# Expert weights fetched in 2 MB transfers into pairs of neighbouring places, with the first loads in a new order

## The chip, the cores and the metric

One Trainium2 chip, one of its cores. The metric is the device time of one execution in microseconds; lower is better. Before and after are compared by the median of several executions.

## The reference, cut to what matters

One step of a one-layer decoder trunk in float32 for 520 tokens (512 of a prompt, 8 samples), width 1024. After a first half (three mixers between an input and an output projection) comes a mixture of 32 experts, of which every token uses 4:

```
logits = xt @ router_w + router_b;  top_v, top_i = top_k(logits, 4);  top_w = softmax(top_v)
for each block of rows with one expert e:
    g = min(x @ w_gate[e] + b_gate[e], 7);  u = clip(x @ w_up[e] + b_up[e], -7, 7)
    y = ((u + 1) * g * sigmoid(1.702 * g)) @ w_down[e] + b_down[e]
x = x + g2 * sum over a token's 4 experts of top_w * y
```

`w_gate`, `w_up` and `w_down` are 1024 x 1024 float32 for each of the 32 experts: 96 matrices of 4 MB, 384 MB in all. Each is read once.

## The kernel before, in words

TensorE does all products. In its first part (to about 285 us in the profile) the kernel computes the mixers, the output projection, the second norm and the routing. Then it goes through 32 expert steps s = 0..31. The expert of a step is the one whose rank by number of tokens is `ORDER[s]`; steps with many tokens have more blocks (`WIDTH` 2 to 5: 64, 64+32, 64+64 and 64+64+32 token rows), so their work on TensorE is longer, while each needs the same 12 MB of weights. Experts 0 and 1 are taken first, so that their weights can be fetched before the routing is known.

**Chunks.** Every matrix comes in four chunks of 1 MB, 8 KB for each of the 128 partitions. Of gate and up, partition p holds the eight rows 8p to 8p + 7, and chunk j brings two neighbouring ones of them (`(p q k) n`, q = 4, k = 2); of down, chunk j brings 256 neighbouring rows, two for each partition (`(q p k) n`). Either way a partition's 8 KB are one run in memory. Chunk numbers run 0..383: gate and up of expert 0 (0 to 7), then in each later step gate, up (8 chunks) and the down matrix of the step before (4 chunks). Chunk n goes to buffer `n % 18` (`NBUF = 18`); `PLACE` says which 8 KB column of memory each buffer is. Twelve of these columns (`raw`) serve the first part's weights and other tiles before, six (`raw2`) lie elsewhere; columns 5, 6, 7 and 1 (`X2_SLOTS`) hold `x2` and broadcasts until the second norm has been written out.

**Issue.** SyncE (SP) issues all weight transfers in one order in one queue, `fetch` and `m_load` (line 489). Chunks 0 to 2 (`EARLY`) are issued once some small results are in; chunks up to 14 (`MIDDLE`) once the output projection is done with its weights (and, for the columns of `X2_SLOTS`, once `x2` has been spilled to DRAM and the norm is ready); 15 to 17 once the routing logits are there. Every later chunk n waits until TensorE has used chunk n - 18: `sp.wait_ge(m_used, n - NBUF + 1)`.

**Use.** In `project` (gate, up) and `down`, TensorE waits for the chunk's own semaphore `m_full[slot]`, multiplies (line 1917, all blocks), and adds one to `m_used`. So chunk follows chunk strictly in order, three passes for a step: gate(s), up(s), down(s-1), with transposes (L1580) and bias products (L1907, L1911) in between.

**Other traffic in these steps.** GpSimd (POOL) gathers the token rows of the next experts from `h2_d` (h_scratch) into `xrow` with indirect DMAs (L673, rows of 4 KB), and scatters results to `y_d` (y_scratch). The first gather starts when the routing of the first two experts is known, after `h2_spill` (the norm's rows written by ScalarE's queue, L975); TensorE's first transpose of the expert steps (L1580, psum<-ident,xrow) waits for it.

Of the kernel before, what the change touches and what calls it, by code (L numbers as in the profile page):

```python
# [26 lines left out]
E, K, DFF = 32, 4, 1024  # L27
# [18 lines left out]
NBUF = 18  # L46
# [44 lines left out]
def blocks_before(s):  # L91

    return sum(len(BLOCKS[w]) for w in WIDTH[:s])
# [8 lines left out]
PRM_LOADS, BC_LOADS = 34, 3  # L102
X2_SLOTS = (5, 6, 7, 1)

EARLY, MIDDLE = 3, 15
PLACE = (15, 16, 17, 0, 2, 3, 8, 9, 10, 11, 6, 7, 4, 1, 5, 12, 13, 14)
CODES = TT * K
FIRST = 96
WIN_ORDER = [1, 2, 3, 5, 0, 4, 6]
# [10 lines left out]
def trunk_program(nc, x_prompt, x_sample, state_pool, state_conv, state_lru_conv, state_lru_h, c_prompt, c_sample,  # L120
# [123 lines left out]
    with ctx:  # L244
        psum = ctx.enter_context(nc.psum_tensor("psum", [P, 8, 512], F32))
        bk = [psum[:, i, :] for i in range(8)]
# [9 lines left out]
        def sem(name):  # L256
            return ctx.enter_context(nc.semaphore(name))
# [6 lines left out]
        m_full = [sem(f"m_full{i}") for i in range(NBUF)]  # L264
        m_used = sem("m_used")
# [94 lines left out]
        def buf(n):  # L360
            at = PLACE[n]
            return raw[:, at, :] if at < 12 else raw2[:, at - 12, :]

        def first_chunk(s):

            return 12 * s - 4 if s else 0
# [31 lines left out]
        def extras(eng, cycle):  # L398

            n = eng.value_load(task_i[0:1, N_AT:N_AT + 1], min_val=0, max_val=XTRA)  # L400
            with eng.Fori(0, XTRA // 8) as q:
                with eng.If(q * 8 < n):
                    with eng.Fori(q * 8, q * 8 + 8) as more:
                        with eng.If(more < n):
                            cycle(more)
            return n
# [16 lines left out]
        def _(sp):  # L423
# [30 lines left out]
            for kind, c in LOADS:  # L454
                kh, n = slice(4 * (c % 2), 4 * (c % 2) + 4), c // 2 + (4 if kind == "mod" else 0)
# [18 lines left out]
                sp.dma_start(bias_raw[E * r:E * r + E, 0, :], moe_b_gate[0, :, h]).then_inc(bias_loaded, 16)  # L474
                sp.dma_start(bias_raw[E * r:E * r + E, 1, :], moe_b_up[0, :, h]).then_inc(bias_loaded, 16)

            def rows_of(mat, e, j):

                down = mat is moe_w_down
                order = "(q p k) n -> p q k n" if down else "(p q k) n -> p q k n"  # L480
                sizes = dict(q=4, k=2)
                if isinstance(e, int):
                    m = mat[0, e].rearrange(order, **sizes)
                    return m[:, j, :, :]
                m = mat[0, bass.ds(e, 1)].rearrange("o " + order.replace("p q k n", "p (o q) k n"), **sizes)
                return m[:, j, :, :]

            def m_load(slot, src):
                sp.dma_start(buf(slot).rearrange("p (k n) -> p k n", k=2), src).then_inc(m_full[slot], 16)  # L489

            def expert(s):

                if s < 2:
                    return s
                return sp.value_load(task_i[0:1, ORDER[s]:ORDER[s] + 1], min_val=0, max_val=E - 1)

            def fetch(n, src):

                if n < EARLY:
                    sp.wait_ge(mod_out[0], 256)  # L500
                    sp.wait_ge(mod_out[1], 256)
                elif n < MIDDLE:
                    sp.wait_ge(chunk_used, C_MOE)
                    if PLACE[n] in X2_SLOTS:
                        sp.wait_ge(x2_spill, 16 * TT)
                        sp.wait_ge(h2_ready, TT)
                elif n < NBUF:
                    sp.wait_ge(logit_ps, TT)
                    sp.wait_ge(mask_done, 1)
                    sp.wait_ge(h2_spill[0], 48)  # L510
                    sp.wait_ge(h2_spill[1], 32)
                else:
                    sp.wait_ge(m_used, n - NBUF + 1)
                m_load(n % NBUF, src)

            before = None
            for s in range(E):
                if s == 2:
                    sp.wait_ge(ids_done, 1)
                e = expert(s)  # L520
                for c in range(8):
                    fetch(first_chunk(s) + c, rows_of((moe_w_gate, moe_w_up)[c // 4], e, c % 4))
                if s:
                    for c in range(4):
                        fetch(first_chunk(s) + 8 + c, rows_of(moe_w_down, before, c))
                before = e
            for c in range(4):
                fetch(first_chunk(E) + c, rows_of(moe_w_down, before, c))
# [1 line left out]
            def extra(q):  # L530

                e = sp.value_load(task_i[0:1, bass.ds(q + E, 1)], min_val=0, max_val=E - 1)
                for c in range(12):
                    sp.wait_ge(m_used, q * 12 + (12 * E + c - 11))
                    m_load((12 + c) % NBUF, rows_of((moe_w_gate, moe_w_up, moe_w_down)[c // 4], e, c % 4))

            sp.wait_ge(all_tables, 1)
            n = extras(sp, extra)


# [1029 lines left out]
        def _(pe):  # L1570
# [322 lines left out]
            def turn_rows(b, rows, full, evicted, count):  # L1893

                pe.wait_ge(x_rows[b], full)
                if evicted is not None:
                    pe.wait_ge(aT_a, evicted)
                    pe.wait_ge(xg_a, count)
                    pe.wait_ge(xg_d, count)
                for k in range(KC):  # L1900
                    last = turn(bk[6 + k // 4][:, (k % 4) * P:(k % 4) * P + rows], xrow[0:rows, b, k:D:KC], rows)
                last.then_inc(xt_ps, 1)

            def bias(out, mat, w):

                if w == 64:
                    mm(out, sel[:, :], btab[:, mat, :], start=True, stop=False)  # L1907
                else:
                    for g4 in range(4):
                        h, c = g4 // 2, 256 * (g4 % 2)  # L1910
                        mm(out[32 * g4:32 * g4 + 32, :], sel[:, 64 * h:64 * h + 32].bitcast(F32),  # L1911
                           btab[:, mat, c:c + 256].bitcast(F32), start=True, stop=False)

            def products(out, w, x, weights, start, stop):

                for g4 in range(128 // w):
                    last = mm(out[w * g4:w * g4 + w, :], x, weights[:, 8 * w * g4:8 * w * g4 + 8 * w],  # L1917
                              start=start, stop=stop)
                return last

            def project(mat, outs, widths, parts, slot0, full):

                for out, w in zip(outs, widths):
                    bias(out, mat, w)
                for j in range(4):
                    slot = (slot0 + j) % NBUF
                    pe.wait_ge(m_full[slot], full(j))
                    for size in (64, 32)[::(1, -1)[j % 2]]:
                        for kk in range(2):
                            for out, w, (x, at_) in zip(outs, widths, parts):  # L1930
                                if w == size:
                                    last = products(out, w, x[:, 2 * j + kk, at_:at_ + w], buf(slot)[:, D * kk:D * kk + D],
                                                    False, j == 3 and kk == 1)
                    last.then_inc(m_used, 1)
# [16 lines left out]
            def turn_act(widths):  # L1951

                for b, w in enumerate(widths):
                    for j in range(w // 16):
                        last = turn(bk[T_BANKS[b]][:, P * j:P * j + P], act_t[:, b, 256 * (j // 2) + j % 2:256 * (j // 2) + 256:2], P)
                    last.then_inc(at_ps, 1)
# [6 lines left out]
                return [(xb, 0), (xb, 64), (xc, 0)][:len(BLOCKS[w])]  # L1963

            def full_at(c0):
                return lambda j: 16 * ((c0 + j) // NBUF + 1)

            turn_rows(0, GATHERS[0][1], 16, None, None)
            for s in range(E):
                c0, widths, before = first_chunk(s), BLOCKS[WIDTH[s]], blocks_before(s)  # L1970
# [31 lines left out]
            c0 = first_chunk(E)  # L2002
            down([down_bank(E - 1, 0)], (64,), c0, full_at(c0))

            def extra(q):

                def full(c):
                    def count(j):
                        slot = (12 + c + j) % NBUF
                        return q * 16 + 16 * (-(-(12 * E - slot) // NBUF) + 1)  # L2010
                    return count

                pe.wait_ge(y_a, q * 2 + ALL_BLOCKS)
                turn_rows(0, P, q * 16 + 16 * (len(range(0, ALL_TURNS, 2)) + 1), q * 2 + ALL_BLOCKS, q + ALL_TURNS)
                pe.wait_ge(xg_a, q + (ALL_TURNS + 1))
                pe.wait_ge(xg_d, q + (ALL_TURNS + 1))
                pe.wait_ge(sel_done, q + (E + 1))
                both = [(xa, 0), (xa, 64)]
                project(0, (bk[4], bk[5]), (64, 64), both, 12, full(0))
                project(1, (bk[0], bk[1]), (64, 64), both, 16, full(4))  # L2020
                pe.wait_ge(act_done, q * 2 + (ALL_BLOCKS + 2))
                turn_act((64, 64))
                pe.wait_ge(aT_a, q * 2 + (ALL_BLOCKS + 2))
                down((bk[2], bk[3]), (64, 64), 20, full(8))
# [64 lines left out]
```

## Time and profile before

| | us |
|---|---|
| median of 3 runs (lowest, highest) | 1341.56 (1337.92, 1342.29) |
| the profiled execution's own time | 1340.82 |
| its span in the trace | 1339.0 |
| TensorE busy | 1253.5 (94%) |
| granted TensorE clock over the span | 0.96 |
| weights' queue (q1): share of the 16 DMA engines | 85.8% |

TensorE's busy time covers nearly the whole span, and the DMA engines are busy nearly the whole span as well, so neither share says which of them sets the end. For that, one looks where TensorE's idle time is and what ended it, and how full the DMA engines are in each stage.

### The profile page before, as it was taken

What the parts mean: (1) busy time and instruction counts of PE and PEld (TensorE: products, weight loads), DVE (VectorE), ACT (ScalarE), POOL (GpSimd) and SP (SyncE); (2) the same over time, 40 slices, a digit from 0 to 9 for tenths busy, and PEclk for the clock granted to TensorE, in tenths of its full rate; (3) what the DMA queues carried; (4) which work ended last, traced back from release to release, by engine and by line L of the source; (5) the groups of instructions that cost most, each with busy time, mean ns of one, the idle gap of its engine ahead of it and who ended that gap; (6) DMA issues with size and microseconds to landing.
All of it is one profiled execution on the core that took longest, in us unless ns stands there. A gap on an engine that the chain in (4) does not pass through costs nothing.

```text
span 1339.0 us, 19202 instructions
## 1 busy us (share of the span) xinstructions
PE 1253.5 (94%) x8190; PEld 560.8 (42%) x8190; DVE 282.6 (21%) x560; ACT 196.2 (15%) x345; POOL 119.1 (9%) x178
## 2 busy tenths in 40 slices
PE   2899979949999999999999999999999999999976
PEld 1687957733333333333333333333333333333322
DVE  0652874684001000001000000001010010001027
ACT  3514252220000110000000000000001000100022
POOL 3010124010100000000000100000001001000000
PEclk8799988959999999999999999999999999999978
DMA  9654469299999999999999999999999999999974
GB/s 317 199 161 165 152 248 303 89 388 398 352 419 421 421 421 421 409 409 422 407 408 419 420 416 420 421 420 401 416 421 420 421 421 420 422 422 421 421 301 177
DMA packets 95077, 486.43 MB, mean 363 GB/s; under 512 B 13650, under 2 KB 21853, under 8 KB 45303
## 3 DMA queue, kind: packets, MB, share of 16 engines
q1 hardware_dynamic: 83306, 461.15, 85.8%
q0 software_dynamic: 8608, 20.82, 4.2%
q10 hardware_dynamic: 3076, 3.22, 0.7%
q8 instruction: 66, 1.08, 0.3%
q14 instruction: 21, 0.16, 0.0%
HBM read 470.26 MB, written 18.04 MB: 365 GB/s over the span
## 4 chain that ended last, share of the span: by engine, by line
PE 81%; DMA 8%; DVE 5%; SPq 3%; ACTq 1%; ACT 1%; issue 1%; DVEq 0%; POOLq 0%
PE psum L1917 61%; PE psum L1580 4%; PE psum L1575 2%; PE psum L1576 2%; PE psum L1577 2%; DMA raw<-in_moe_w_gate 2%; DMA raw<-in_moe_w_down 2%; SPq L489 2%; PE psum L1907 2%; DMA bd_x<-in_lru_wx 1%; ACTq L766 1%; DMA raw<-in_ada_w 1%; PE psum L2038 1%; PE psum L1737 1%; PE psum L1642 1%
## 5 line engine op out<-in xcount | busy, mean ns | idle before, releaser
L1917 PE MATMUL psum<-raw,xb 128*64 128x512 f32 (+1 forms) x1920 | 304.4, 513 | 0.4 <-DMA raw<-in_moe_w_gate 0.4
L1917 PE MATMUL psum<-raw,aT 128*64 128x512 f32 (+1 forms) x1728 | 301.1, 532 | 3.7 <-DMA raw<-in_moe_w_down 3.5
L1917 PE MATMUL psum<-raw,xa 128*64 128x512 f32 x1280 | 283.5, 595 | 0.0
L1501 DVE TENSOR_SCALAR act_t<-psum 128x512 f32<-128x512 f32 (+1 forms) x46 | 28.4, 642 | 873.4 <-PE psum L1917 873.4
L1917 PEld LDWEIGHTS psum<-raw,xb 128*64 128x64 f32 (+1 forms) x1920 | 100.4, 126 | 189.4 <-issue 175.4
L1917 PEld LDWEIGHTS psum<-raw,aT 128*64 128x64 f32 (+1 forms) x1728 | 98.4, 129 | 187.3 <-issue 167.0
L1917 PEld LDWEIGHTS psum<-raw,xa 128*64 128x64 f32 x1280 | 88.2, 137 | 169.7 <-issue 169.7
L673 POOL DMA_INDIRECT xrow<-h_scratch,gidx x24 | 27.5, 1144 | 464.6 <-PE psum L1580 430.5
L989 ACT ACTIVATE glu<-psum 128x512 f32<-128x512 f32 (+1 forms) x46 | 24.2, 559 | 292.1 <-PE psum L1917 292.1
L1575 PE MATMUL psum<-hT_hi,w_hi 128*128 128x260 f32 x208 | 59.3, 285 | 0.0
L1576 PE MATMUL psum<-hT_lo,w_hi 128*128 128x260 f32 x208 | 58.9, 283 | 0.0
L1577 PE MATMUL psum<-hT_hi,w_lo 128*128 128x260 f32 x208 | 58.7, 282 | 0.0
L685 POOL DMA_INDIRECT y_scratch<-yst_a,sunit x23 | 22.9, 994 | 305.7 <-ACT yst_a L1004 260.4
L1004 ACT ACTIVATE yst_a<-psum 128x512 f32<-128x512 f32 (+1 forms) x27 | 14.5, 558 | 210.3 <-PE psum L1917 210.3
L1642 PE MATMUL psum<-raw,cT 128*9 128x128 f32 x768 | 30.7, 324 | 13.1 <-DMA raw<-in_ada_w 13.1
L1575 PEld LDWEIGHTS psum<-hT_hi,w_hi 128*128 128x128 f32 x208 | 39.1, 188 | 1.1 <-issue 1.1
L1577 PEld LDWEIGHTS psum<-hT_hi,w_lo 128*128 128x128 f32 x208 | 39.2, 189 | 0.0
L1576 PEld LDWEIGHTS psum<-hT_lo,w_hi 128*128 128x128 f32 x208 | 39.1, 188 | 0.1
L1580 PE MATMUL psum<-ident,xrow 128*128 128x128 f32 (+2 forms) x192 | 27.9, 289 | 8.9 <-DMA xrow<-h_scratch,gidx 8.9
L1907 PE MATMUL psum<-btab,sel 128*128 128x512 f32 x76 | 34.3, 478 | 1.1 <-ACT xb L1014 1.1
L1580 PEld LDWEIGHTS psum<-ident,xrow 128*128 128x128 f32 (+2 forms) x192 | 23.5, 198 | 27.7 <-issue 18.7
L1580 PEld LDWEIGHTS psum<-ident,act_t 128*128 128x128 f32 x168 | 22.5, 208 | 27.0 <-issue 25.2
(398 smaller groups left out, 925.2 us busy)
## 6 DMA issues: line engine op xcount, KB each, us to landing
raw<-in_moe_w_gate SPq DMA_DIRECT2D x128, 1024.0 KB, 26.2
raw<-in_moe_w_up SPq DMA_DIRECT2D x128, 1024.0 KB, 26.7
raw<-in_moe_w_down SPq DMA_DIRECT2D x128, 1024.0 KB, 26.9
raw<-in_ada_w SPq DMA_DIRECT2D x24, 1024.0 KB, 8.3
raw<-in_w_in SPq DMA_DIRECT2D x7, 1024.0 KB, 11.5
x<-in_x_prompt SPq DMA_DIRECT2D x2, 2048.0 KB
raw<-in_w_out SPq DMA_DIRECT2D x4, 1024.0 KB, 13.1
yrow_a<-y_scratch SPq DMA_DIRECT2D x2, 2048.0 KB, 10.9
```

The source lines that it names most:

```text
L489: sp.dma_start(buf(slot).rearrange("p (k n) -> p k n", k=2), src).then_inc(m_full[slot], 16)
L673: g.indirect_dma_start(out=out, out_offset=None, in_=h2_d, in_offset=bass.IndirectOffsetOnAxis(ap=index, axis=0), bounds_check=h2_last, oo ...
L685: g.indirect_dma_start(out=out, out_offset=bass.IndirectOffsetOnAxis(ap=index, axis=0), in_=src, in_offset=None, bounds_check=last, oob_is ...
L989: ac.activation(glu[:, b, 0:bank.shape[1]], bank, ACT.Gelu_apprx_sigmoid).then_inc(glu_done, 1)
L1501: v.tensor_scalar(act_t[:, b, 0:bank.shape[1]], bank, 8.0, -6.0, ALU.min, ALU.max).then_inc(u_done, 1)
L1575: mm(out, lhi, rhi, start=start, stop=False)
L1576: mm(out, lhi, rlo, start=False, stop=False)
L1577: return mm(out, llo, rhi, start=False, stop=stop)
L1580: return nc.tensor.transpose(out, src, ident[0:rows, 0:rows])
L1642: last = mm(outs[j], cT[:, 4 * kh + k, :], raw[:, slot, 512 * k + P * j:512 * k + P * j + P], start=False, stop=(kh == 1 and k == 3))
L1907: mm(out, sel[:, :], btab[:, mat, :], start=True, stop=False)
L1917: last = mm(out[w * g4:w * g4 + w, :], x, weights[:, 8 * w * g4:8 * w * g4 + 8 * w], start=start, stop=stop)
```

## The change

Gate and up chunks are fetched two at a time: one transfer of 2 MB puts 16 KB, one run in memory, into each partition, in two neighbouring columns. A partition now holds four consecutive rows of the matrix for a pair (`q=2, k=4`), instead of two for each of two chunks. `PLACE` is reordered so that buffers 0-1, 2-3, ... 16-17 are neighbours. Down chunks stay single, 1 MB. A pair counts on the semaphore of its first buffer; `filled_by` and `fills` work out which semaphore and which count TensorE waits for. A pair waits until both chunks that it overwrites have been used. `EARLY` and `MIDDLE` go from 3 and 15 to 2 and 14, and the first loads are issued in the order of `FIRST_LOADS`. TensorE's products, their order and `m_used` stay.

```diff
-EARLY, MIDDLE = 3, 15
-PLACE = (15, 16, 17, 0, 2, 3, 8, 9, 10, 11, 6, 7, 4, 1, 5, 12, 13, 14)
+EARLY, MIDDLE = 2, 14
+PLACE = (16, 17, 2, 3, 0, 1, 10, 11, 8, 9, 6, 7, 4, 5, 12, 13, 14, 15)
+FIRST_LOADS = (0, 2, 6, 8, 4, 10, 12, 14, 16, 17)
...
+        def buf2(n):
+            at = PLACE[n]
+            whole = raw[:, at:at + 2, :] if at < 12 else raw2[:, at - 12:at - 10, :]
+            return whole.rearrange("p a (k n) -> p (a k) n", k=2)
+        def is_down(c):
+            return c >= first_chunk(E) or (c >= 8 and (c - 8) % 12 >= 8)
+        def filled_by(c):
+            return c % NBUF if is_down(c) else c % NBUF // 2 * 2
+        def fills(c):
+            firsts = [b for b in range(c + 1) if is_down(b) or b % 2 == 0]
+            return sum(filled_by(b) == filled_by(c) for b in firsts)
...
-            def rows_of(mat, e, j):
+            def rows_of(mat, e, j, single=False):
...
-                sizes = dict(q=4, k=2)
+                sizes = dict(q=4, k=2) if down or single else dict(q=2, k=4)
...
+            def m_load2(slot, src):
+                sp.dma_start(buf2(slot), src).then_inc(m_full[slot], 16)
             def fetch(n, src):
+                double = not is_down(n)
...
-                    if PLACE[n] in X2_SLOTS:
+                    if PLACE[n] in X2_SLOTS or (double and PLACE[n] + 1 in X2_SLOTS):
...
-                    sp.wait_ge(m_used, n - NBUF + 1)
-                m_load(n % NBUF, src)
+                    sp.wait_ge(m_used, n - NBUF + (2 if double else 1))
+                if double:
+                    m_load2(n % NBUF, src)
+                else:
+                    m_load(n % NBUF, src)
+            for n in FIRST_LOADS:
+                if is_down(n):
+                    fetch(n, rows_of(moe_w_down, 0, n - 16))
+                else:
+                    fetch(n, rows_of((moe_w_gate, moe_w_up)[n % 8 // 4], n // 8, n % 4 // 2))
...
-                for c in range(8):
-                    fetch(first_chunk(s) + c, rows_of((moe_w_gate, moe_w_up)[c // 4], e, c % 4))
+                for c in range(0, 8 if s > 1 else 0, 2):
+                    fetch(first_chunk(s) + c, rows_of((moe_w_gate, moe_w_up)[c // 4], e, c % 4 // 2))
+                for c in range(2 if s == 1 else 0, 4):
+                    fetch(first_chunk(s) + 8 + c, rows_of(moe_w_down, before, c))
...
-                    pe.wait_ge(m_full[slot], full(j))
+                    pe.wait_ge(m_full[filled(slot0 + j)], full(j))
...
-                return lambda j: 16 * ((c0 + j) // NBUF + 1)
+                return lambda j: 16 * fills(c0 + j)
```

A loop for experts with more tokens than their blocks hold (`extra`) keeps single chunks; its loads and its counts are adapted.

## Rows read from the trace of the kernel before

**Rows 1.** The page: TensorE's busy time, and the DMA engines in 40 slices.

```profile
PE 1253.5 (94%) x8190; PEld 560.8 (42%) x8190; DVE 282.6 (21%) x560; ACT 196.2 (15%) x345; POOL 119.1 (9%) x178
...
DMA  9654469299999999999999999999999999999974
GB/s 317 199 161 165 152 248 303 89 388 398 352 419 421 421 421 421 409 409 422 407 408 419 420 416 420 421 420 401 416 421 420 421 421 420 422 422 421 421 301 177
```

**Rows 2.** Waits of TensorE from 299 to 1284 us: us in total, times, longest.

```profile
PE psum L1917 <- DMA raw<-in_moe_w_down: 3.5, 5, 1.1
...
PE psum L1917 <- DMA raw<-in_moe_w_gate: 0.4, 1, 0.4
```

**Rows 3.** Timeline of TensorE at its waits: start, us, instruction, [idle before].

```profile
294.50 1.55 PE L1580 MATMUL psum<-ident,xrow 96*128 96x96 f32 x8 [8.88 <-DMA xrow<-h_scratch,gidx]
...
640.55 1.94 PE L1917 MATMUL psum<-raw,aT 128*64 128x512 f32 x8 [0.80 <-DMA raw<-in_moe_w_down]
...
644.37 11.26 PE L1917 MATMUL psum<-raw,xb 128*64 128x512 f32 x96 [0.40 <-DMA raw<-in_moe_w_gate]
...
1270.16 1.94 PE L1917 MATMUL psum<-raw,aT 128*64 128x512 f32 x8 [0.37 <-DMA raw<-in_moe_w_down]
...
1283.56 1.94 PE L1917 MATMUL psum<-raw,aT 128*64 128x512 f32 x8 [0.66 <-DMA raw<-in_moe_w_down]
```

**Rows 4.** The chain that ended last: its transfers (start, us from issue to landing).

```profile
285.24 9.22 DMA xrow<-h_scratch,gidx
...
614.63 29.70 DMA raw<-in_moe_w_gate
```

**Rows 5.** Windows: busy us of each engine, clock, DMA share, GB/s.

```profile
325.00:375.00 50.00, 48.24 (x376) 18.51 (x376) 4.90 (x12) 5.07 (x11) 4.64 (x4) 1.00 0.94 358
375.00:640.00 265.00, 264.74 (x1282) 93.38 (x1278) 20.78 (x40) 22.50 (x40) 18.30 (x18) 1.00 1.01 418
```

**Rows 6.** DMA packets of two short windows: 614 to 617, then 1296 to 1302 us.

```profile
DMA packets 171, 1.26 MB, mean 421 GB/s; under 512 B 17, under 2 KB 17, under 8 KB 17
...
DMA packets 173, 2.57 MB, mean 429 GB/s; under 512 B 16, under 2 KB 16, under 8 KB 16
```

**Rows 7.** SyncE's queue: weight transfers issued (start, us, count), and its waits.

```profile
219.88 47.82 SPq L489 DMA_DIRECT2D raw<-in_moe_w_gate  x4
267.75 2.39 SPq L489 DMA_DIRECT2D raw<-in_moe_w_up  x4
...
282.10 24.42 SPq L489 DMA_DIRECT2D raw<-in_moe_w_down  x4
...
370.77 6.19 SPq L489 DMA_DIRECT2D raw<-in_moe_w_down  x4
...
604.92 8.95 SPq L489 DMA_DIRECT2D raw<-in_moe_w_down  x4
...
SPq L506 <- DMA x_scratch<-x: 5.7, 1, 5.7
SPq L510 <- DMA h_scratch<-h2f: 2.3, 1, 2.3
```

**Rows 8.** DMA queues from 289.9 to 292.4 us, during the first gather.

```profile
q1 hardware_dynamic: 68, 0.55, 71.4%
q0 software_dynamic: 69, 0.23, 30.3%
```

**Rows 9.** Gathers, issue to landing: of 350 to 370, and of 310 to 1250 us.

```profile
xrow<-h_scratch,gidx POOLq DMA_INDIRECT x1, 5.2
...
DMA to landing us min/median/max: 5.2/8.7/10.3
```

**Rows 10.** Step 29: issue of its gate chunks, their landing, and TensorE's arrival.

```profile
1155.53 8.26 SPq L489 DMA_DIRECT2D raw<-in_moe_w_gate  x4
...
raw<-in_moe_w_gate SPq DMA_DIRECT2D x2, 1024.0 KB, 28.2
...
1184.79 13.95 PE L1917 MATMUL psum<-raw,xb 128*64 128x512 f32 x64
```

More of the change, by code:

```diff
@@ L362, in buf, with fills_in_all @@
             return raw[:, at, :] if at < 12 else raw2[:, at - 12, :]
+        def buf2(n):
[9 more added lines that the diff above has]
+            return sum(filled_by(b) == filled_by(c) for b in firsts)
+        def fills_in_all(slot):
+            return sum(filled_by(b) == slot for b in range(12 * E) if is_down(b) or b % 2 == 0)
         def first_chunk(s):
@@ L512, in fetch @@
                 else:
-                    sp.wait_ge(m_used, n - NBUF + 1)
-                m_load(n % NBUF, src)
-            before = None
-            for s in range(E):
+                    sp.wait_ge(m_used, n - NBUF + (2 if double else 1))
[8 more added lines that the diff above has]
+                    fetch(n, rows_of((moe_w_gate, moe_w_up)[n % 8 // 4], n // 8, n % 4 // 2))
+            before = 0
+            for s in range(1, E):
                 if s == 2:
@@ L520, in _ @@
                 e = expert(s)
-                for c in range(8):
-                    fetch(first_chunk(s) + c, rows_of((moe_w_gate, moe_w_up)[c // 4], e, c % 4))
-                if s:
-                    for c in range(4):
-                        fetch(first_chunk(s) + 8 + c, rows_of(moe_w_down, before, c))
+                for c in range(0, 8 if s > 1 else 0, 2):
+                    fetch(first_chunk(s) + c, rows_of((moe_w_gate, moe_w_up)[c // 4], e, c % 4 // 2))
+                for c in range(2 if s == 1 else 0, 4):
+                    fetch(first_chunk(s) + 8 + c, rows_of(moe_w_down, before, c))
                 before = e
@@ L534, in extra @@
                     sp.wait_ge(m_used, q * 12 + (12 * E + c - 11))
-                    m_load((12 + c) % NBUF, rows_of((moe_w_gate, moe_w_up, moe_w_down)[c // 4], e, c % 4))
+                    m_load((12 + c) % NBUF, rows_of((moe_w_gate, moe_w_up, moe_w_down)[c // 4], e, c % 4, single=True))
             sp.wait_ge(all_tables, 1)
@@ L1919, in products, with project @@
                 return last
-            def project(mat, outs, widths, parts, slot0, full):
+            def project(mat, outs, widths, parts, slot0, full, filled=lambda c: filled_by(c)):
                 for out, w in zip(outs, widths):
@@ L2009, in count @@
                         slot = (12 + c + j) % NBUF
-                        return q * 16 + 16 * (-(-(12 * E - slot) // NBUF) + 1)
+                        return q * 16 + 16 * (fills_in_all(slot) + 1)
                     return count
@@ L2018, in extra @@
                 both = [(xa, 0), (xa, 64)]
-                project(0, (bk[4], bk[5]), (64, 64), both, 12, full(0))
-                project(1, (bk[0], bk[1]), (64, 64), both, 16, full(4))
+                project(0, (bk[4], bk[5]), (64, 64), both, 12, full(0), lambda c: c % NBUF)
+                project(1, (bk[0], bk[1]), (64, 64), both, 16, full(4), lambda c: c % NBUF)
                 pe.wait_ge(act_done, q * 2 + (ALL_BLOCKS + 2))
```

## The prediction

> **What bounds the kernel now.** I read the page first. TensorE is busy 94% of the span, and from the twelfth of the 40 slices to the thirty-eighth the DMA engines are full as well, at about 420 GB/s [rows 1]. Two resources that are both full look like a tie, so the next views are TensorE's waits and the fill of the DMA engines by stage. From 299 us, when the expert steps have begun, to 1284 us TensorE waited for weights 3.5 + 0.4 = 3.9 us in all, in six waits [rows 2]. The reader is to see the size of this number: whatever the change does for the transfers, on TensorE it can give back 3.9 us of 985, 0.3% of the kernel. The timeline shows where: 0.80 and 0.40 us at 640 and 644 us, where a run of narrow steps has eaten the stock of loaded chunks, and the other 2.7 us, four waits for down of 0.37 to 1.12 us, from 1270 us to the end [rows 2, 3]. The transfers at these places took 29.7 us from issue to landing [rows 4], against 5 to 10 us for gathers [rows 9]: they stood in a queue that is never empty. So the expert steps are bound by TensorE, with two places (640 to 645 us, and the end) where the transfers are just as late.
>
> The windows say when the transfers are held back. From 325 to 375 us they run at 358 GB/s and a share of 0.94: all 18 places are taken and SP waits for TensorE. From 375 us the share is 1.01, at 418 GB/s with the gathers in it [rows 5]. From there on a saved microsecond of transfer is a microsecond of stock.
>
> In front of the steps stands one more wait for a transfer, on the path for certain: TensorE waits 8.88 us for the first gather of token rows [rows 3], which took 9.22 us from issue at 285.24 us to landing [rows 4]. It runs beside the first weight loads, which SP issued from 267.75 us on [rows 7].
>
> **Part 1: the rate of a transfer.** 8 KB runs: a window with only weight loads has 1.26 MB in 171 packets, 17 of them the small ones of the semaphores, so 8.2 KB each, at 421 GB/s. The final stage happens to load result rows of 16 KB in one run: 2.57 MB in 173 packets, 16 small, so 16.4 KB each, at 429 GB/s [rows 6]. A chunk of 1.049 MB takes 2.49 us, a pair now 4.98 us, and after the change 2.097/0.429 = 4.89 us: 0.09 us less. (Lower end: nothing, if the weights gain nothing from the longer run.) 40 chunks (to up of step 3) are issued before the down chunks of 370.77 us [rows 7]; of the 344 behind them two thirds come in pairs, 115 pairs: 10.3 us less transfer by the end. The down chunks late at 640 us are those issued from 604.92 us on, chunks 136 to 139; up to them 33 pairs: 3.0 us less by the tight place.
>
> The Trainium skill, page DMA: Bandwidth & Descriptors, section Bandwidth, gives 341 GB/s for a transfer of 1 MB and 425 for 16 MB, and in the section Anatomy of one DMA a fixed part of about 2 us per transfer. It is given there for GpSimd's transfers. If it stood between queued transfers, 1 MB each would run at some 240 GB/s and 2 MB at some 310, and all 3.9 us of waits would go. The trace shows 421 at 1 MB each [rows 6], so nothing of this kind is to be won here.
>
> **Part 2: a pair wants two free places.** From 325 to 375 us, where places are what is short, a pair is issued when the second of its places is free, one chunk later than the first would be now. At the end of this stage up to 1 MB less has been transferred: 0 to 2.5 us; I take 2.0, since the transfers run at 85% of their full rate in this stage (358 of 421) and catch a little up. Later places are no longer short, since chunks wait 28 us in the queue anyway [rows 10].
>
> **Part 3: a pair lands as one.** TensorE can start on the first half only when both are there, 2.49 us later than now. Where it has a lead, this costs nothing. At 644 us it has none: now the first gate chunk lands at 614.63 + 29.70 = 644.3 us, the second about 2.5 us later, 646.8. After the change, counted from the same start of the steps: 646.8 + 2.0 (part 2) - 3.0 (part 1) = 645.8 us. TensorE is there at 643.97 (644.37 less its wait) - 0.80, since the down chunk before it is no longer late (now 0.80 late, then 2.0 - 3.0 earlier): 643.2 us. It waits 2.6 us, where the two waits are 1.2 now: +1.4 us. The steps just behind (13, also narrow in stock) may add some tenths; I add 0.4. At step 29 the gate chunks are issued at 1155.53 us and land 28.2 us later, at 1183.7, one microsecond ahead of TensorE at 1184.79 [rows 10]; by then part 1 has brought some 9 us, so a pair isn't late there. At the end, where down chunks are single, the transfers are 10.3 - 2.0 = 8.3 us earlier, and the 2.7 us of waits go. Sum on TensorE: +1.4 + 0.4 - 2.7 = -0.9 us. More speed can't give more than -3.9. Without any gain in rate, the down chunk is 2.8 us late at 640 us and the pair as late again: +4.4 at the tight place, -1.0 at the end where the stall has made stock: +3.4 us.
>
> **Part 4: the first gather among packets of twice the size.** During the gather the DMA engines take a gather row and a weight run in turn: from 289.9 to 292.4 us, 69 packets on the gathers' queue and 68 on the weights' [rows 8]; 2.5 us for 4.3 rounds of 16 engines, 0.58 us a round. The gather's 96 rows are six rounds. After the change, SP will have issued chunks 2-3, 6-7 and 8-9 by about 272 us and the next after its wait of 5.7 us [rows 7], so the queue holds pairs from 267 to about 300 us, as it holds single chunks now. Each round gets longer by half of 4.89/8, 0.31 us: +1.8 us. That is the low end from this mechanism. The high end comes from the spread of the gathers: one between 350 and 370 us, when the engines were not full [rows 5], took 5.2 us [rows 9], so 4.0 of the 9.22 are waiting behind weights; twice that is +4.0. I take +2.9. No cover here: TensorE stands idle for it.
>
> On this the Trainium skill, same page, section Queues, rings and completion order, says that an engine "round-robins between the queue rows it has work for, at *packet* granularity", a packet being 9 to 17 descriptors. Then a gather would wait out one transfer's whole share on the engine, 4.89 us instead of 2.49: +2.4. The rows show one run for one row; the sum comes out alike.
>
> **Part 5: costed at nothing.** The early load is 2 MB instead of 3 at 219.88 us, and one more MB stands in the batch from 267 us, which then takes 16 x 2.49 = 40 us and is done at 307 instead of 305; gate and up of the first step are among the first 8 MB, landed by 290, and TensorE can't use them before the gather has landed. The reordered loads wait for the same spills (5.7 and 2.3 us [rows 7]), with 6 MB queued in front, 14.7 us of work, so that the engines don't run dry. If the last small norm row (landed before the down chunks could be issued at 282.10, wanted by POOL at 285.24) meets longer packets too, it has 3 us of cover. Places are all full by 325 us either way, which wipes out this order. SP issues 125 or so fewer instructions, but it isn't on the path. The later gathers (8.7 us) and scatters get some 2 to 4 us longer, under steps of some 30 us (985 us by 32). The tail from 1285 us holds no weight load.
>
> **Sum.** -0.9 (parts 1 to 3) + 2.9 (part 4) = +2.0 us on the profiled execution's own 1340.8: 1342.8. The median before is 0.7 us above that execution, so I give 1343.0.
>
> **The rivals.**
> *Slower: 16 KB runs are no faster for the weights* (or the hardware cuts them into 8 KB packets, so that the change doesn't do what it says). For it: the 429 GB/s come from another tensor in a stage without any other traffic. Against: both windows are at a full share, and the step from 421 to 429 is just what a fixed cost per packet gives. Then +3.4 + 2.9 = +6.3: 1347.1; with packets cut, +3.4 alone: 1344.2. It decides (over +4.0) once a pair saves less than about 0.03 us.
> *Slower: the gather suffers more.* If waiting behind weights is 6 instead of 4 of its 9.2 us, or the last norm row runs out of its cover: +5 to +6 at the start, 1345 to 1347. It decides from +4.9 us on the gather, a landing after 14 us.
> *Faster: the gather isn't slowed, and the rate gain covers the pair's late landing.* Weights' and gathers' queues would have to share by bytes instead of in turn; against it stand rows 8. Then -0.9 to -3.9: 1337 to 1340. To be seen as faster it needs nearly all of it.
>
> **Chances.** A measurement of this kernel can tell 0.3%, 4.0 us, from no change. The forecast, between -3 and +4 us: 0.64. No gain in rate: 0.14; a slower gather: 0.13; faster: 0.09. Of the first rival a part stays under 4 us, of the forecast a part lies over it. Faster by over 0.3%: 0.08; within: 0.65; slower: 0.27. The range takes in the forecast (1339 to 1345) and reaches up to the first slower rival: 1338.5 to 1348.
>
> **What the profile after would show.** Right: weights' windows from 375 us at 424 to 427 GB/s; the first gather landing 11 to 13 us after issue and TensorE's first transpose at 297 us; one wait of 2 to 3 us for gate at about 647 us, and no waits for down at the end. Wrong: GB/s unchanged; waits at steps that had a lead, which would say that places are short for longer than I think; TensorE's first transpose at 294.5 us; or a time outside the range from something in the first 285 us, which I have put at nothing.

## The result and the profile after

The changed kernel is slower: its median is 1347.53 us (1343.02 to 1349.91, 20 runs) against 1341.99 us (1337.92 to 1348.22, 20 runs), ratio 1.0034 with a 95% interval of 1.0026 to 1.0043. By the ratio that is 4.6 us (3.5 to 5.8), by the medians 5.5. The forecast was +2.0 us, 1343.0. The profiled execution of after took 1346.84 us, its span is 1345.1 us, 6.1 us more than before. Its page, to be laid beside [rows 1]:

```profile
PE 1256.3 (93%) x8190; PEld 562.3 (42%) x8190; DVE 282.7 (21%) x560; ACT 196.1 (15%) x345; POOL 118.9 (9%) x178
...
DMA  9554469199899999999999999998999999999984
GB/s 317 197 158 151 167 227 290 79 387 407 323 409 424 425 426 424 411 407 425 411 405 425 425 417 415 422 425 328 416 408 425 425 425 424 423 425 427 424 332 182
```

Most slices that stood at 419 to 422 GB/s stand at 424 to 427 now. Four that stood at 407 to 409 (the seventeenth, eighteenth, twentieth and twenty-first) gained nothing (405 to 411). And one slice, the twenty-eighth, falls from 401 to 328; it comes up again under part 2 below. The transfers are faster, as forecast, if by less, and the kernel is not.

Where the time went is in TensorE's rows. Its waits for transfers from 299 to 1290 us in the trace of after:

```profile
PE psum L1617 <- DMA xrow<-h_scratch,gidx: 11.3, 1, 11.3
PE psum L1954 <- DMA raw<-in_moe_w_gate: 3.1, 1, 3.1
...
PE psum L1954 <- DMA raw<-in_moe_w_up: 1.0, 1, 1.0
PE psum L1954 <- DMA raw<-in_moe_w_down: 0.3, 1, 0.3
```

The sum for weights, 4.4 us, is close to the 3.9 of before [rows 2]. What differs is where they stand. The timeline of TensorE after, to be laid beside [rows 3]:

```profile
299.44 1.54 PE L1617 MATMUL psum<-ident,xrow 96*128 96x96 f32 x8 [11.26 <-DMA xrow<-h_scratch,gidx]
...
303.80 13.14 PE L1954 MATMUL psum<-raw,xb 128*64 128x512 f32 x96
...
636.34 3.65 PE L1954 MATMUL psum<-raw,xa 128*64 128x512 f32 x16 [1.04 <-DMA raw<-in_moe_w_up]
...
646.66 1.94 PE L1954 MATMUL psum<-raw,aT 128*64 128x512 f32 x8 [0.31 <-DMA raw<-in_moe_w_down]
...
653.20 12.59 PE L1954 MATMUL psum<-raw,xb 128*64 128x512 f32 x96 [3.12 <-DMA raw<-in_moe_w_gate]
...
666.71 11.12 PE L1954 MATMUL psum<-raw,xb 128*64 128x512 f32 x96
...
1276.34 7.04 PE L1954 MATMUL psum<-raw,aT 128*64 128x512 f32 x32
...
1284.78 7.09 PE L1954 MATMUL psum<-raw,aT 128*64 128x512 f32 x32 [0.19 <-issue]
```

and two more rows of before:

```profile
298.87 12.72 PE L1917 MATMUL psum<-raw,xb 128*64 128x512 f32 x96
...
656.56 11.12 PE L1917 MATMUL psum<-raw,xb 128*64 128x512 f32 x96
```

Three things are to be seen. The first gather is waited for 11.26 us instead of 8.88. All three waits for weights stand at 636 to 653 us, 4.47 us where there were 1.20, and the waits at the end are gone. And behind the wait of 3.12 us the same 96 products take 12.59 us, 1.47 more than the 11.12 of the next 96: the granted clock of TensorE from 653 to 657 us is 0.60, where the stretches of 4 us before and behind have 0.97 and 1.00. So most of that stretch ran at the lower of the two levels (1.2 GHz of 2.4).

```profile
325.00:375.00 50.00, 48.24 (x401) 19.00 (x399) 7.54 (x16) 4.47 (x10) 4.64 (x4) 1.00 0.89 341
375.00:640.00 265.00, 263.96 (x1274) 92.49 (x1270) 18.82 (x36) 22.60 (x40) 17.21 (x17) 1.00 1.01 421
...
900.00:960.00 60.00, 60.00 (x370) 21.66 (x370) 5.45 (x11) 4.52 (x9) 1.95 (x2) 1.00 0.90 370
...
653.00:657.00 4.00, 3.80 (x18) 1.06 (x22) 0.00 (x0) 0.00 (x0) 0.00 (x0) 0.60 0.98 414
```

The first two windows answer to [rows 5]: 341 for 358 GB/s in the stage in which places are short, 421 for 418 behind it.

The transfers on the chain, to be laid beside [rows 4]:

```profile
287.78 11.61 DMA xrow<-h_scratch,gidx
...
610.79 42.36 DMA raw<-in_moe_w_gate
```

The second row is the late pair: it lands at 653.15 us, and the products at 653.20 us start with it. The single chunk at this place in before took 29.70 us.

The span's 6.1 us come apart like this. The gather is issued 2.54 us later (287.78 against 285.24). Nearly all of this isn't the change's doing: SP issues the first expert weights at 222.07 us in after and at 219.88 in before [rows 7], 2.19 us later before any changed transfer is on its way.

```profile
222.07 48.05 SPq L523 DMA_DIRECT2D raw<-in_moe_w_gate  x2
```

From issue to landing the gather takes 2.39 us more (11.61 - 9.22). The first 96 products take 0.4 us more (13.14 against 12.72). At 636 to 666 us TensorE loses 4.47 - 1.20 + 1.47 = 4.7 us. The end gives back 3.8 us: the up products of step 12 begin 10.15 us later than before (666.71 against 656.56), and the last products of the steps end only 6.4 us later (1284.78 + 7.09 against 1283.56 + 1.94 [rows 3]). The tail is 0.3 us shorter.

### The profile page after: what moved, and what is told of

Same layout as the page of the kernel before. It is cut to its first block, busy times and chain, and to the rows that moved or that the text cites. A ratio compares the mean times of both kernels' runs of the same rounds, so it can differ in the third digit from the quotient of the medians.

```text
span 1345.1 us, 18891 instructions
## 1 busy us (share of the span) xinstructions
PE 1256.3 (93%) x8190; PEld 562.3 (42%) x8190; DVE 282.7 (21%) x560; ACT 196.1 (15%) x345; POOL 118.9 (9%) x178
## 4 chain that ended last, share of the span: by engine, by line
PE 85%; DMA 7%; DVE 4%; ACTq 1%; ACT 1%; issue 1%; SPq 1%; DVEq 0%; POOLq 0%
PE psum L1954 64%; PE psum L1617 5%; DMA raw<-in_moe_w_gate 3%; PE psum L1612 2%; PE psum L1613 2%; PE psum L1614 2%; PE psum L1944 2%; PE psum L1679 1%; DMA bd_x<-in_lru_wx 1%; ACTq L803 1%; PE psum L1774 1%; PE psum L2075 1%; DMA raw<-in_ada_w 1%; DMA xrow<-h_scratch,gidx 1%; PE psum L1948 1%
## 6 DMA issues: line engine op xcount, KB each, us to landing
raw<-in_w_in SPq DMA_DIRECT2D x7, 1024.0 KB, 11.6
```

## Experiments

Ratios are to runs of the kernel before on the same chips; where two runs stood on different chips, they are compared by their ratios and not by their medians. "Gather" is the first gather's time from issue to landing, "waits" are TensorE's for weights in the steps, both from the profiled execution, one for each run.

| run | ratio (95%) | gather, us | waits, us |
|---|---|---|---|
| after | 1.0034 (1.0026 to 1.0043) | 11.61 | 4.4 |
| r2 order and places, no pairs | 1.0001 (0.9991 to 1.0012) | 8.7 | 4.5 |
| r1 first 18 chunks single | 1.0027 (1.0014 to 1.0040) | 8.89 | 4.2 |
| r3 pairs of two 8 KB transfers | 1.0050 (1.0032 to 1.0068) | 9.41 | 6.4 |
| r7 steps 12, 13 single | 0.9996 (0.9984 to 1.0008) | 11.6 | 1.0 |
| r5 after, gather before chunk 10 | 0.9998 (0.9986 to 1.0009) | 7.14 | 4.0 |
| r6 = r5 + r7 | 0.9969 (0.9957 to 0.9981) | 6.94 | 1.3 |
| r4 before, gather before chunk 10 | 0.9971 (0.9960 to 0.9982) | 4.83 | 3.9 |
| r4b the same again | 0.9968 (0.9950 to 0.9986) | 4.7 | 3.6 |
| r8 gather first, pairs where stock is | 0.9953 (0.9940 to 0.9967) | 7.58 | 0 |
| r8b the same again | 0.9959 (0.9943 to 0.9975) | 8.1 | 0.5 |
| r9 as r8, no pairs | 0.9988 (0.9976 to 1.0000) | 8.4 | 3.5 |
| r10 as r8, gather before chunk 4 | 0.9972 (0.9959 to 0.9986) | 4.12 | 4.8 |

My theory at the start: the loss is partly the first gather among longer packets and partly the pair that lands as one at the tight place. Rivals: the order of first loads; chance before the steps; long packets that cost in the steps as well.

**The order alone (r2).** All chunks single, in the new places and order. (Here and below `is_single` names the chunks that are fetched alone, 1 MB each; in the changed kernel these are the down chunks. Where the first 18 chunks are single, in r1, r2, r8, r9 and r10, `FIRST_LOADS` names both halves of each pair, in the same order.)

```diff
-            return is_down(c)
+            return c >= 0
```

> The new places and the new order of first loads alone, every chunk a single transfer of 8 KB. Theory (order and places cost nothing, all places are full by 325 us anyway): the time of before within 0.1%, gather 9.2 us, waits for weights on TensorE 3.9 us as before. Rival (something of the loss of 5.5 us lies in the order, among it the 2.4 us by which the gather was issued later in the changed kernel's profile): ratio 1.001 to 1.002 and the gather issued at 287 to 288 us again.

1342.16 us, ratio 1.0001. The order costs nothing, as costed, within the 0.1% that the interval leaves. The gather was issued at 286.9 us here. Over the 14 profiled executions of this study the first gather is issued at 284.7 to 288.1 us; the two of r8 and r8b, one kernel, at 286.7 and 284.7. So the 2.54 us of before and after are within what the part before the steps varies by from run to run, and 2.19 of them are there before the order of loads can act. The rival that the order explains them falls.

**Short packets beside the gather only (r1).**

```diff
-            return is_down(c)
+            return is_down(c) or c < NBUF
```

> The changed kernel with its first 18 chunks as single 1 MB transfers of 8 KB runs (in the order 0 to 3, 6 to 9, 4, 5, 10 to 17), pairs from chunk 18 on. Theory (a third to a half of the loss is the first gather among 16 KB packets): the gather lands 9.0 to 9.6 us after issue as before instead of 11.6, TensorE's steps start 2.4 us earlier counted from the gather's issue, and the kernel is 2 to 3 us faster than the changed one, 2 to 3 us slower than before (ratio about 1.002). Rival (the gather's delay is chance, and the whole loss is pairs landing late): no change against the changed kernel, ratio 1.0035.

1345.12 us. The chain has the gather back at its old time:

```profile
286.24 8.89 DMA xrow<-h_scratch,gidx
```

so it is the pairs in front of it that cost 2.4 to 2.7 us. r3 below narrows that to their 16 KB runs: with runs of 8 KB the gather takes 8.66 to 9.41 us (before, r1, r2, r3), with runs of 16 KB 11.60 and 11.61 (r7, after). The total was 1 us better than after by the ratios, within their intervals, so the price of this part on the kernel's time isn't shown by r1 alone. In the steps r1 waited about as long as after, and lost more behind its wait: the same 96 products take 14.01 us, 2.9 more than the 11.12 at the full clock, where after lost 1.5. That takes back about half of the 2.7 us that the gather had won.

```profile
PE psum L1968 <- DMA raw<-in_moe_w_gate: 3.3, 1, 3.3
PE psum L1968 <- DMA raw<-in_moe_w_up: 0.5, 1, 0.5
PE psum L1968 <- DMA raw<-in_moe_w_down: 0.4, 1, 0.4
...
648.02 14.01 PE L1968 MATMUL psum<-raw,xb 128*64 128x512 f32 x96 [3.30 <-DMA raw<-in_moe_w_gate]
```

**Pairs with short packets (r3).** Everything of the change but the 16 KB run.

```diff
-                sp.dma_start(buf2(slot), src).then_inc(m_full[slot], 16)
+                for h in range(2):
+                    sp.dma_start(buf(slot + h).rearrange("p (k n) -> p k n", k=2),
+                                 src[:, 2 * h:2 * h + 2, :]).then_inc(m_full[slot], 16)
```

> The changed kernel with each pair fetched by two transfers of 1 MB and 8 KB runs that count on one semaphore: waits for two places and landing as one stay, packets of 16 KB go. Theory (long packets cost 2.4 us at the gather and win transfer rate in the steps; waiting for two and landing as one cost on their own): gather back to about 9.2 us, GB/s from 375 us on back to 418, waits of TensorE for weights 6 to 9 us with the ones at the end back, so 1 to 3 us slower than before plus the landing: ratio 1.002 to 1.005. Rival (the 16 KB packets are what costs in the steps too): waits back to 3.9 us, ratio 1.000 to 1.001.

1348.28 us, ratio 1.0050 by six runs. That is in the theory's range, but the waits at the end, which I expected back, stay away. The rival (long packets cost in the steps) falls, since without them the kernel is no faster. Beside r2, where only the pairing is missing, waiting for two places and landing as one cost 0.5%, 6.6 us (4 to 9 by the intervals). The profiles show 5.2 of them: 1.9 us more of waits and 3.3 of slow stretches behind two of them. The rate is back to that of before, and a second place has become tight, at 556 us, again with a slow stretch behind it (15.65 us for 64 products that take 13.95 in the row behind):

```profile
325.00:375.00 50.00, 48.24 (x383) 18.64 (x375) 5.39 (x12) 4.47 (x10) 4.65 (x4) 1.00 0.94 360
375.00:640.00 265.00, 263.07 (x1263) 92.45 (x1262) 18.97 (x37) 22.60 (x40) 17.24 (x17) 0.99 1.01 418
...
288.06 9.41 DMA xrow<-h_scratch,gidx
...
556.54 15.65 PE L1969 MATMUL psum<-raw,xb 128*64 128x512 f32 x64 [1.93 <-DMA raw<-in_moe_w_gate]
572.12 0.73 PE L1959 MATMUL psum<-btab,sel 128*128 128x512 f32 x2
572.78 13.95 PE L1969 MATMUL psum<-raw,xb 128*64 128x512 f32 x64
...
651.86 12.75 PE L1969 MATMUL psum<-raw,xb 128*64 128x512 f32 x96 [2.50 <-DMA raw<-in_moe_w_gate]
```

**The gather first (r4, r5).** SP holds back chunk 10 and all behind it until the first gather has landed; in the kernel before (r4) and in the changed one (r5).

```diff
             def fetch(n, src):
+                if n == 10:
+                    sp.wait_ge(x_rows[0], 16)
```

> The kernel before with one wait more on SP: chunk 10 and what is behind it are issued when the first gather has landed. Theory (the gather waits behind weights, and the transfers held back are made up by 325 us since all places are full then): the gather lands 5 to 6.5 us after issue instead of 9.2, the steps start 3 to 4 us earlier, weights are late nowhere new, and the kernel is 3 to 4 us faster than before (ratio 0.9975). Rival (stock is lost and comes back as waits at 640 us and at the end): same time as before, with 3 to 4 us more waiting for weights.

> The changed kernel with SP holding back chunks 10 and behind until the first gather has landed. Theory (the gather's delay is weights in front of it, and the transfers held back are made up while all places are full): the gather lands about 5 us after issue instead of 11.6, the loss of 4 to 5 us at the tight place near 645 us stays, and the kernel is 5.5 to 6.7 us faster than the changed one: 1341 us, ratio 0.999 (0.998 to 1.0). Rival (a shorter stock makes the pairs late earlier): less than 4 us gained, more waits for gate before 640 us.

r4: 1338.05 us, ratio 0.9971, as forecast. r5: 1342.92 us, ratio 0.9998, in the forecast's range of 0.998 to 1.0, 0.36% or 4.8 us better than after. That is a little less than the 5.5 to 6.7 us of the theory, and so is the gather's part in the chain:

```profile
284.95 7.14 DMA xrow<-h_scratch,gidx
```

7.1 us and not 5: of the chunks issued from 267 us on, 8 MB stand in front of chunk 10 in the new order, where there were 7, so weights still ran beside the gather. (r4's is 4.83.) The tight place stayed as it was. r4 has 3.9 us of waits for weights, as before; r5 has the same kind of row as after:

```profile
645.50 12.75 PE L1970 MATMUL psum<-raw,xb 128*64 128x512 f32 x96 [3.95 <-DMA raw<-in_moe_w_gate]
```

**Single transfers at the tight place (r7, and r6 with the gather first).**

```diff
-            return is_down(c)
+            return is_down(c) or 140 <= c < 164
```

> The changed kernel with gate and up of steps 12 and 13 (chunks 140 to 163) as single transfers. Theory (the loss in the steps is the pair that lands as one where the stock is used up): the wait before step 12 falls from 3.1 to 0.5 to 1.5 us, the loss against the start of the steps there from 4.8 to 2 to 3 us, and the kernel is 2 to 3 us faster than the changed one, ratio 1.0015 to 1.002. Rival (the last transfers set the end, so the stall in the middle costs nothing): no gain, ratio 1.0035, waits for down at the end back.

> Both edits: gather alone, and steps 12 and 13 single. Theory: the two gains add up, 8 to 9 us faster than the changed kernel, 1338 to 1339 us, ratio 0.9970 to 0.9980, so equal to or a little faster than the kernel before with the gather alone (0.9971). Rival (they do not add up): ratio 0.999.

r7: 1342.89 us, ratio 0.9996. That is 0.38% or 5.1 us under after (some 3 to 7 by the intervals; 4.7 by the spans of the two traces), more than the theory's 2 to 3 us, and the rival (the stall costs nothing, since the last transfers set the end) falls. The wait is short, and the 96 products behind it take 11.22 us: the clock doesn't fall any more.

```profile
648.77 11.22 PE L1968 MATMUL psum<-raw,xb 128*64 128x512 f32 x96 [1.02 <-DMA raw<-in_moe_w_gate]
...
1279.00 7.09 PE L1968 MATMUL psum<-raw,aT 128*64 128x512 f32 x32 [0.19 <-issue]
```

The last row stands for the end: no wait for down there. With 16 of its 384 chunks changed from pairs to singles (gate and up of two steps; their down chunks were single already), the changed kernel is level with before. r6, both edits: 1339.34 us, ratio 0.9969 by six runs. The gains are 0.36% and 0.38% alone and 0.65% together, so within the intervals they add up.

**Pairs only where there is stock (r8), and what they bring (r9).** r8 is r5's hold with single transfers up to chunk 43 and for gate and up of steps 9 to 13.

```diff
-            return is_down(c)
+            return is_down(c) or c < 44 or 104 <= c < 164
```

> Gather alone, and pairs only where there is stock: single transfers for chunks up to 43 (the stage in which all places are full) and for gate and up of steps 9 to 13 (chunks 104 to 163), pairs elsewhere. Theory (waiting for two places costs 2 us of stock in the stage before 375 us, and pairs cost nothing where chunks land early, while they still bring a higher rate before 540 us and behind 710 us): waits of TensorE for weights under 2 us in all, ratio 0.995 to 0.9965, the fastest of all, 1 to 3 us under the kernel before with the gather alone. Rival (pairs bring no rate that counts): 0.9971, equal to the kernel before with the gather alone.

1337.65 us, ratio 0.9953 by five runs: faster than before, and in its profiled execution TensorE doesn't wait for weights at all in the steps. It was measured again on one chip with r4 and with r9, which is r8 without pairs:

> As the previous best (gather alone, pairs where there is stock), but with no pairs at all: every chunk a single transfer, same places and order of first loads. Asks what the pairs still bring. Theory (16 KB runs save some 0.04 us a pair, enough to take the waits at the end away): 2.5 to 3.5 us slower than with the pairs, waits for down at the end back at 2 to 3 us in all. Rival (pairs bring nothing that counts): the same time within 1 us.

> The previous best again, on the chip of its neighbours in this call: ratio 0.9953 as before within 0.001.

> The kernel before with the gather alone again, beside the best: ratio 0.9971 within 0.001, 1.5 to 3 us slower than the best.

r8b again 0.9959 (1337.68 us), r4b 0.9968 (1337.78 us): the two can't be told apart by these intervals, and the 1.5 to 3 us between them are not shown. What r8b wins over r4b in the steps it has lost at the gather, which takes 8.1 us there and 4.7 in r4b. Pairs where there is stock, with r4's shorter gather, were not tried. r9 is at 0.9988 (0.9976 to 1.0000, 1341.44 us), 3.8 us slower than r8b by medians, just above the range that I gave; the two intervals only just part. Its waits for weights are back:

```profile
PE psum L1970 <- DMA raw<-in_moe_w_down: 2.7, 4, 0.9
PE psum L1970 <- DMA raw<-in_moe_w_gate: 0.8, 1, 0.8
```

So pairs do bring something where chunks land early. The windows of 375 to 640, 660 to 900 and 960 to 1240 us, first r9, then r8:

```profile
375.00:640.00 265.00, 265.00 (x1284) 93.47 (x1280) 20.79 (x40) 22.50 (x40) 18.30 (x18) 1.00 1.01 418
660.00:900.00 240.00, 240.00 (x1694) 89.45 (x1690) 17.71 (x38) 19.47 (x41) 20.93 (x19) 1.00 1.01 418
960.00:1240.00 280.00, 280.00 (x1458) 100.08 (x1456) 21.79 (x43) 25.61 (x47) 19.31 (x19) 1.00 1.01 420
```

```profile
375.00:640.00 265.00, 265.00 (x1285) 93.71 (x1283) 20.77 (x40) 22.48 (x40) 18.25 (x18) 1.00 1.01 420
660.00:900.00 240.00, 240.00 (x1690) 89.39 (x1688) 17.70 (x38) 19.45 (x41) 20.90 (x19) 1.00 1.01 421
960.00:1240.00 280.00, 280.00 (x1458) 100.10 (x1456) 21.77 (x43) 25.60 (x47) 19.27 (x19) 1.00 1.01 423
```

**The gather wholly alone (r10).** r8 with the hold at chunk 4.

```diff
-                if n in (10,):
+                if n in (4,):
```

> The best with SP holding back from chunk 4 on instead of from chunk 10 on, so that 6 MB instead of 8 are in front of the gather. Theory (in the best the queue still held weights up to 291 us, and the gather took 7.6 us against 4.9 in the kernel before with its gather alone): the gather lands about 5 us after issue, 2.0 to 2.7 us less, ratio 0.993 to 0.994. Rival (up of the first step, chunks 4 to 7, now comes too late, or what is left is not weights): no gain, a wait for up before 315 us.

1339.83 us, ratio 0.9972, and my forecast (0.993 to 0.994) was wrong: it is no faster than r8, and slower by the middle values, though its interval overlaps that of r8b on the same chip. The gather did land in 4.12 us, 3.5 us sooner after its issue than in r8. But of that nothing was left:

```profile
325.00:375.00 50.00, 50.00 (x377) 18.44 (x375) 2.76 (x6) 3.70 (x8) 3.39 (x3) 1.00 1.01 420
...
641.38 1.94 PE L1970 MATMUL psum<-raw,aT 128*64 128x512 f32 x8 [2.74 <-DMA raw<-in_moe_w_down]
```

In the kernel before, the stage from 325 to 375 us had room for (421 - 358) x 50 / 421 = 7.5 us of transfers more. r10 kept the engines idle so long that this stage is full (420 GB/s, share 1.01) and the stock was still smaller: 4.8 us of waits, 3.9 of them at the tight place. The rival had no gain right, and the place wrong: there was no wait before 315 us. In r4 the same window has 403 GB/s; its hold fits in.

## Why the prediction was right and wrong

The sign was right, the time lay in the range, and both places of the loss were named. But the +2.0 us came out as 4.6, 0.65 of the chances stood on no change beyond 0.3%, and the result lies just beyond it. The steps that failed are the rate (part 1) and the price of the tight place (part 3), where TensorE's clock was put at nothing. Step by step:

- **What bounds it: right.** r7 shows it best: without the stall in the middle of the steps the kernel is faster by the stall's length.
- **Part 4, the gather: right in kind, near in size.** +2.9 forecast, +2.39 measured. The rows of its queues in after, from 292.4 to 295.4 us, show again one gather row for one run:

```profile
q1 hardware_dynamic: 50, 0.82, 86.1%
q0 software_dynamic: 49, 0.17, 16.9%
```

  3.1 rounds in 3 us, 0.98 us a round instead of 0.58 [rows 8]; six rounds of 0.40 more are 2.4 us. The low end (+1.8) took the round's growth too small (0.31), the high end the gather's waiting (4.0 us; r4 and r10, nearly or wholly without weights beside it, take 4.83 and 4.12 of the 9.22). The 2.9 itself was a choice between the two. Not foreseen: the first 96 products took 0.4 us more. That isn't tied to the length of the idle time before them: in r5 they take 12.05 us behind 6.79 us of idle, in r4 13.35 behind 4.49.

  The Trainium skill (DMA: Bandwidth & Descriptors, Queues, rings and completion order) says that an engine drains a whole packet of one queue before it turns to the next; the prediction's estimate by it was +2.4 too. The time agrees, the rows don't: in after each microsecond from 292 to 297 us has 16 to 19 packets of the weights' queue and 16 or 17 of the gathers', about one of each for each of the 16 engines, so here they take turns run by run.
- **Part 2, two free places: right as far as shown.** 2.0 us forecast. (375 - 360) x 50 / 421 = 1.8 us by r2 and r3, and (358 - 341) x 50 / 421 = 2.0 by before and after. In r2 this window is:

```profile
325.00:375.00 50.00, 48.24 (x376) 18.69 (x374) 5.39 (x12) 5.06 (x11) 4.64 (x4) 1.00 0.97 375
```

  These windows lie still while the steps start at 294.5 (before), 295.6 (r2), 297.5 (r3) and 299.4 us (after). r2, with no pairs, has 17 GB/s more than before, so the numbers are rough.

  I missed that the same stage comes again at 900 to 960 us, behind the widest step (370 GB/s, in before 410), which is the low slice of the page. It cost nothing: the gate pair issued at 931.82 us is used at 974.43 us, and transfers issued there land after 10 to 13 us at the median.
- **Part 1, the rate: too large.** I took 0.09 us a pair from the bare 429 GB/s of the final stage, 3.0 us by the tight place (counted out there are 112 and 32 pairs, not 115 and 33, which changes 0.3 us at most). The window of 375 to 640 us went from 418 to 421, 0.7%, 1.9 us of 265, and not to the 424 to 427 that I had named; r8 against r9 has 0.5 to 0.7%. The page shows where it went: most slices gained about 1%, some nothing, among them the four at 407 to 409. Gathers alone don't make these four, since nearly every slice holds some: in before the rate falls to 330 GB/s from 548 to 552 us, beside the gather issued at 544.00, and stays at 415 to 421 from 452 to 464, beside the one issued at 453.25. The same four are low in r2, r7 and r8 too. What sets these gathers apart, and why nothing is gained beside them, stays open.
- **Part 3, landing as one: right in kind, too small.** I had 2.6 us of waits at the tight place; it was 4.47. With 1.1 us less gained by then, the up pair before step 12's gate was late as well (1.04). Missing altogether was TensorE's clock: 1.47 us behind the wait of 3.12. So the place cost +4.7 and not +1.4 + 0.4. Of the 2.9 us between them 1.5 are the clock, 1.1 by estimate the rate, and 0.3 stay open.
- **The end: right.** -2.7 forecast, 3.8 given back: the four waits (2.7), and 1.1 us by which the 64 products that they broke up had taken longer (3.60 + 1.94 + 1.94 and 3.85 + 1.94 + 1.94 us, now 7.04 and 7.09). I had put it down to the rate alone. In r7, which has the rate and no long stall, these waits are gone; in r3, which has the stalls and no gain in rate, too. So in the changed kernel either would have done.
- **Part 5: right** by r2 (1.0001).
- **The base.** 1342.8 is for the profiled execution, and before's median was 0.7 us above that, so the sum gives 1343.5 for a median; I wrote 1343.0.

The sum with measured terms: 2.4 + 0.4 + 4.7 - 3.8 - 0.3 = 3.4 us, against 4.6 by the ratio (3.5 to 5.8). What is left over, about 1 us, stays open; a single profile of either kernel varies by more than that. That the first rival (no gain in rate) would have given +6.3 and r3, which is just this case without the gather's part, measured +6.7 (4.3 to 9.1), says that I had the price of landing as one too small there too (+3.4).

## What to carry to other kernels

Where two engines are both full, look for the few places where the stock of loaded data is used up: what a larger transfer wins in rate counts only there and at the end, and there its later landing costs at once. Fetch in large pieces where data lands early and in small ones where it lands just in time; with this and the gather first, pairs gain 0.3% (r8b beside r9), while the whole change loses as much. And for a small transfer that an engine stands idle for, the bulk can be held back, as long as the stage behind it has room for what was held back (r4 gains 0.3%, r10 overdraws). That part needs no pairs: r4 alone is as fast as r8b within the intervals.

## What was not expected of the hardware

- Behind a wait of 3.1 us the granted clock of TensorE fell to 0.60 for 4 us and cost 1.5 us; products were slow as well after 3.30 us (r1, 14.01 for 11.12 us, 0.50 for 4 us and 0.75 for 4 more), 3.95 us (r5, 12.75), 2.50 us (r3, 12.75) and even 1.93 us (r3, 15.65 for 13.95). After 1.02 us (r7) it didn't fall, nor after 1.91 us in r2 or 2.74 us in r10. So the length of the wait alone doesn't decide. The five that were followed by a slow stretch are waits for gate, right behind the short transposes and bias products at the start of a step; those of 1.91 and 2.74 us stand between the products of one down matrix. That the place is what decides is argued from these rows and not tested. The row of r2, to be laid beside that of r3 at 556 us:

```profile
643.37 1.94 PE L1968 MATMUL psum<-raw,aT 128*64 128x512 f32 x8 [1.91 <-DMA raw<-in_moe_w_down]
...
646.71 11.12 PE L1968 MATMUL psum<-raw,xb 128*64 128x512 f32 x96
```

- Long packets slow other queues' small transfers: gathers in the steps landed in 8.7 us at the median before, and in 9.9 us after (12.4 at most instead of 10.3). With pairs of 8 KB runs (r3) it is 8.7 us again, 10.5 at most, so it is the run of 16 KB and not the pairing.
